# A mixture-of-experts encoder layer on one core: one-time work of the early experts gathered into the first five, and the branch over extra blocks right behind them

## The chip, the cores and the metric

The kernel runs on one core of a Trainium2 chip. The metric is the device time of one execution in microseconds, lower is better. Before the change the median of three runs is 1279.49 us (1279.22 to 1279.97).

## What is computed

One encoder layer over 256 tokens of width 1024, all in float32: a mixer (differential attention beside a two-way state space scan), cross attention over 256 memory tokens, and a mixture of experts, each added to the residual stream; then a final RMSNorm. The change touches the mixture of experts alone:

```python
t = rms_norm(h)                                   # 256 tokens x 1024
top_v, top_i = top_k(t @ w_router + b_router, 4)  # 32 experts
gates = softmax(top_v)
for each expert e and the tokens routed to it:
    hid  = xb @ w_e1[e] + b_e1[e]                 # 1024 -> 2048
    gate = min(hid[:, :1024], 7); lin = clip(hid[:, 1024:], -7, 7)
    act  = gate * sigmoid(1.702 * gate) * (lin + 1)
    y    = act @ w_e2[e] + b_e2[e]                # 1024 -> 1024
h = h + sum over experts of gate_weight * y
out = rms_norm(h, norm_final_g)
```

Each expert has 8 MB in `w_e1` and 4 MB in `w_e2`, and every expert's weights are read once, some 400 MB in all.

## The kernel before

Everything ahead of the experts (mixer, cross attention, router) is straight-line code for the five engines, ordered by semaphores. Then come 32 blocks, one for each expert, of up to 64 tokens. An expert that more than 64 tokens chose would get further blocks, the extra blocks, up to 15 over all experts. How many there are (`n_extra`) is only known on the chip; with the inputs used here there are none, and 32 blocks run.

**Weights.** The weights of an expert are six chunks of 2 MB: four of `w_e1` (numbers 0 to 3) and two of `w_e2` (4 and 5). SyncE issues them in order (`load_block`, `load_chunk`, L308) into a ring of 10 slots, with an eleventh place (`spare`) that serves twice at the start. A slot's next load waits for TensorE to be done with the chunk ten (early on eleven) places earlier (`freed_by`; semaphores `m_w1u` and `m_w2u`). SyncE's program is not touched by the change.

**A block on TensorE** (`block_of`, L1175): four times `hidden_chunk` (16 product instructions of 128x512, L1147), with the hidden bias behind chunk 0 (L1138); then `gather` of the tokens of the next block (L1057), transposes of the gate weights (L574), `scatter` of the previous block's output into the accumulators (L1073), transposes of the hidden values, transposes of the next tokens; then twice `output_part` with a `w_e2` chunk (16 product instructions each, L1169). ScalarE and VectorE do the activation, the selection matrices and the copies between.

**One-time work of the early blocks** is slipped between the chunks of certain blocks by `behind_chunk(early, j)`: two products that add the residual of token tile 1 to its accumulator (`add_residual`, L1023; blocks 3 and 4), the tables of the extra blocks and the transposed gate weights (`extra_block_tables`, block `TABLES_AT` = 5), four products that add the output bias (`add_bias`, L1079; blocks 6 and 7, behind chunks 0 and 2), and the spreading of the final norm's gain (`spread_gain`, L1086; block `GAIN_AT` = 8, behind its first `w_e2` chunk). Behind the latter ScalarE copies the gain out (L1307), and TensorE waits for that copy at the block's end.

**Loops and the branch.** A loop body holds `ROUND` = 5 blocks, since 30 chunks are three turns of the ring. On TensorE blocks 0 to 9 are written out, blocks 10 to 19 are a loop of two rounds, then `n_extra` is loaded into a register (L1274) and a branch follows (L1275). Each of its two arms holds `last_blocks()`: a loop of two rounds (blocks 20 to 29) and the blocks 30 and 31 in an order of their own. The first arm goes on with the code of the extra blocks; the second one is taken here. VectorE writes out blocks 0 to `TABLES_AT` - 1 and ScalarE blocks 0 to `GAIN_AT`, then each has a loop of one block.

Of the kernel before, what the change touches and what calls it, by code (L numbers as in the profile page):

```python
# [42 lines left out]
CHUNKS = W1_CHUNKS + W2_CHUNKS  # L43
ROUND = 5
ROUNDS = NE // ROUND
BRANCH_AT = 4
TABLES_AT, GAIN_AT = 5, 8


C_ID = 0  # L50
# [33 lines left out]
def build(nc, T, out):  # L84

    ctx = ExitStack()
    with ctx:
        def sb(name, cols, parts=P, dt=F32):
            return ctx.enter_context(nc.sbuf_tensor(name, [parts, cols], dt))
# [56 lines left out]
        early = sb("early", 512)  # L146
# [138 lines left out]
        def chunk_at(q, r, j):  # L285

            opening = isinstance(q, int) and q == 0
            n, use = place_at(opening, r, j)
            return n, 16 * use if opening else (q * (CHUNKS * ROUND // RING) + use) * 16
# [9 lines left out]
        def last_chunk_at(b, j):  # L299

            n = LAST.index((b, j)) - len(SPARE_USES)
            return n % RING, (ROUNDS * (CHUNKS * ROUND // RING) + n // RING + 1) * 16
# [259 lines left out]
        def _(pe):  # L562
# [458 lines left out]
            def add_residual(t, n, start):  # L1021

                pe.matmul(pt[(PA, PB)[t]][:, 512 * n:512 * (n + 1)], ident, h3[:, t, 512 * n:512 * (n + 1)],  # L1023
                          start=start, stop=False)
# [52 lines left out]
            def add_bias(t, n):  # L1077

                pe.matmul(pt[(PA, PB)[t]][:, 512 * n:512 * (n + 1)], gT[:, P * t:P * (t + 1)],  # L1079
                          be2[:, 512 * n:512 * (n + 1)], start=False, stop=False)  # L1080

            def spread_gain():
# [4 lines left out]
                                     start=True, stop=True)  # L1087
                last.then_inc(S["ctp"], 1)

            def behind_chunk(early, j):  # L1090

                if early == 3 and j == 3:
                    add_residual(1, 0, False)
                elif early == 4 and j == 1:
                    add_residual(1, 1, False)
                elif early == TABLES_AT:
                    extra_block_tables(j)
                elif early in (6, 7) and j in (0, 2):
                    add_bias(early - 6, j // 2)

            readers[PD] = []
            pe.wait_ge(m_sel, 1)
# [13 lines left out]
            def extra_block_tables(j):  # L1116

                if j == 0:
                    pe.wait_ge(S["ctv"], 1)
                    pe.matmul(pt[PD][0:NE, 0:1], con[0:NE, C_TRI:C_TRI + NE], nbx[:, 0:1], start=True, stop=True).then_inc(S["ctp"], 1)  # L1120
                elif j == 1:
                    pe.wait_ge(S["ctv"], 2)
                    pe.matmul(pt[PD][:, 64:64 + 2 * EXTRA + 1], ones[0:NE, :], blk[:, :], start=True, stop=True).then_inc(S["ctp"], 1)
                elif j == 2:
                    pe.wait_ge(S["ovi"], 1)
                    pe.wait_ge(S["gdv"], NT)
                    for t in range(NT):
                        last = turn(pt[PD][0:NE, 128 + P * t:128 + P * (t + 1)], gate[:, t, :])
                    last.then_inc(S["ctp"], 1)
                else:  # L1130
                    pe.wait_ge(S["gda"], 1)

            def add_hidden_bias():

                for b in range(2):
                    for g in range(2):
                        i = NE * (2 * b + g)
                        pe.matmul(pt[PC][SLOTS * g:SLOTS * (g + 1), 512 * b:512 * (b + 1)], ecol[i:i + NE, :],  # L1138
                                  be1[i:i + NE, :], start=False, stop=False)

            def hidden_chunk(n, j):

                for k in (2 * j, 2 * j + 1):
                    for b in range(2):
                        for g in range(2):
                            c = 2048 * (k % 2) + D * b + 512 * g
                            last = pe.matmul(pt[PC][SLOTS * g:SLOTS * (g + 1), 512 * b:512 * (b + 1)], xT[:, k % 4, k // 4],  # L1147
                                             ring_slot[n][:, c:c + 512], start=(k == 0), stop=(k == KD - 1))
                last.then_inc(m_w1u, 1)
# [25 lines left out]
            def block_of(it, q, r, early=None):  # L1175

                pe.wait_ge(m_xT, 1 if early == 0 else it + 2)
                for j in range(W1_CHUNKS):
                    n, loaded = chunk_at(q, r, j)
                    pe.wait_ge(s_chunk[n], loaded)  # L1180
                    if early == 0 and j == 1:
                        pe.wait_ge(m_xT, 2)
                    if j == 1:
                        add_hidden_bias()
                    hidden_chunk(n, j)
                    behind_chunk(early, j)

                pe.wait_ge(m_sel, it + 2)
                gather()

                if early != 0:
                    pe.wait_ge(m_y, it)
                turn_weights(it)

                if early != 0:
                    pe.wait_ge(m_gs, it)
                    scatter(False, start=(1,) if early == 1 else ()).then_inc(m_sc, 1)

                turn_hidden(it)
                pe.wait_ge(m_xn, it + 2)  # L1200
                turn_block(xgn_early if early == 0 else xgn)

                pe.wait_ge(m_hT, it + 1)
                pe.wait_ge(m_gs, it + 1)
                for g in range(W2_CHUNKS):
                    n, loaded = chunk_at(q, r, W1_CHUNKS + g)
                    pe.wait_ge(s_chunk[n], loaded)
                    output_part(n, g, hT, 512, range(4))
                    if early == GAIN_AT and g == 0:
                        spread_gain()  # L1210
                if early == GAIN_AT:
                    pe.wait_ge(S["acopy"], 7)

            def last_blocks():

                with pe.Fori(BRANCH_AT, ROUNDS) as q:
                    for r in range(ROUND):
                        block_of(q * ROUND + r, q, r)
                a, b = NE - 2, NE - 1
                pe.wait_ge(m_xT, a + 2)  # L1220
                for j in range(W1_CHUNKS):
                    n, loaded = last_chunk_at(0, j)
                    pe.wait_ge(s_chunk[n], loaded)
                    if j == 1:
                        add_hidden_bias()
                    hidden_chunk(n, j)
                pe.wait_ge(m_sel, a + 2)
                gather()
                pe.wait_ge(m_y, a)
                turn_weights(a)  # L1230
                pe.wait_ge(m_gs, a)
                scatter(False).then_inc(m_sc, 1)
                turn_hidden(a)
                pe.wait_ge(m_xn, a + 2)
                turn_block()

                pe.wait_ge(m_hT, a + 1)
                pe.wait_ge(m_xT, b + 2)
                for j in range(W1_CHUNKS):
                    n, loaded = last_chunk_at(1, j)  # L1240
                    pe.wait_ge(s_chunk[n], loaded)
                    if j == 1:
                        add_hidden_bias()
                    hidden_chunk(n, j)
                pe.wait_ge(m_gs, a + 1)
                turn_weights(b)

                for g in range(W2_CHUNKS):
                    n, loaded = last_chunk_at(0, W1_CHUNKS + g)
                    pe.wait_ge(s_chunk[n], loaded)  # L1250
                    output_part(n, g, hT_wait, 0, range(4))
                    if g == 0:
                        turn_hidden(b)

                pe.wait_ge(m_hT, b + 1)
                pe.wait_ge(m_gs, b + 1)
                for g in range(W2_CHUNKS):
                    n, loaded = last_chunk_at(1, W1_CHUNKS + g)
                    pe.wait_ge(s_half[g], 16)
                    output_part(n, g, hT, 512, (0, 1))  # L1260
                    if g == 0:
                        pe.wait_ge(m_y, a + 1)
                        scatter(False, gsc=gsc_wait).then_inc(m_sc, 1)
                    pe.wait_ge(s_chunk[n], loaded)
                    output_part(n, g, hT, 512, (2, 3))

            for q in range(2):
                for r in range(ROUND):
                    block_of(q * ROUND + r, q, r, early=q * ROUND + r)
            with pe.Fori(2, BRANCH_AT) as q:  # L1270
                for r in range(ROUND):
                    block_of(q * ROUND + r, q, r)
            pe.wait_ge(S["ovi"], 1)
            n_extra = pe.value_load(idx[0:1, NE + EXTRA + 1:NE + EXTRA + 2], min_val=0, max_val=EXTRA)  # L1274
            with pe.If(n_extra > 0):  # L1275
# [948 lines left out]
```

## Time and profile before

| | us |
|---|---|
| median of three runs | 1279.49 |
| the profiled execution, whole | 1279.54 |
| its span (first to last instruction) | 1277.6 |
| around the span | 1.9 |
| TensorE busy in the span | 1241.8 |
| VectorE, ScalarE, GpSimd busy | 410.7, 170.8, 113.3 |

The span is cut into 40 slices of 31.9 us on the page. The experts begin at 365 us, in slice 11 (counted from 0), and last to the end. The chain that ended last is made of TensorE for 83% and of DMA for 12%. TensorE's busy time includes the time in which one matmul fills while another drains, so that a busy TensorE isn't one at its peak. The mean granted clock of TensorE is 0.997.

### The profile page before, as it was taken

How to read it: one execution, taken by the hardware profiler on the slowest of the kernel's cores; microseconds unless marked ns; L12 is line 12 of the kernel's file. 1: busy time of each engine (PE TensorE's matmuls, PEld its weight loads, DVE VectorE, ACT ScalarE, POOL GpSimd, SP SyncE). 2: the span in 40 equal slices, each digit the busy share in tenths (PEclk: the TensorE clock that was granted, in tenths of full speed). 3: DMA queues.
4: the chain of work that ended last, by engine and by line, in shares of the span. 5: the costliest groups of instructions: out<-in, count | busy, mean ns of one | idle time of the engine just before them, and what ended most of it. 6: DMA issues, size and time to landing. Idle time of an engine off the chain costs nothing.

```text
span 1277.6 us, 15129 instructions
## 1 busy us (share of the span) xinstructions
PE 1241.8 (97%) x6111; PEld 559.7 (44%) x6111; DVE 410.7 (32%) x845; ACT 170.8 (13%) x299; POOL 113.3 (9%) x107
## 2 busy tenths in 40 slices
PE   8999999999999999999999999999999999999997
PEld 4478886759543333333333333333333333333332
DVE  6789685367432111111121111121111112111111
ACT  2043333011221000000100000000000000000002
POOL 4599400020000000000000000000000000000000
PEclk9999999999999999999999999999999999999999
DMA  8743476692789999999999999999999999999996
GB/s 247 183 165 132 99 137 243 216 311 86 305 349 429 426 427 428 429 426 428 428 428 427 426 428 428 428 428 429 427 426 427 428 427 429 428 428 429 428 427 255
DMA packets 55603, 455.96 MB, mean 357 GB/s; under 512 B 4840, under 2 KB 7088, under 8 KB 30720
## 3 DMA queue, kind: packets, MB, share of 16 engines
q1 hardware_dynamic: 52736, 450.80, 86.0%
q0 software_dynamic: 1664, 3.90, 2.3%
q10 hardware_dynamic: 1152, 0.52, 0.3%
q8 instruction: 40, 0.66, 0.2%
q14 instruction: 11, 0.09, 0.0%
HBM read 453.07 MB, written 1.61 MB: 356 GB/s over the span
## 4 chain that ended last, share of the span: by engine, by line
PE 83%; DMA 12%; DVE 2%; ACT 2%; issue 1%; SPq 0%; DVEq 0%
PE pt L1147 29%; PE pt L1169 16%; PE pt L609 9%; PE pt L596 4%; PE pt L1073 4%; PE pt L574 4%; PE pt L636 4%; PE pt L1057 4%; DMA ring<-in_w_e 3%; DMA stage<-in_w_e 3%; DMA low<-in_w_e 3%; PE pt L1138 2%; PE pt L646 2%; DMA stage<-in_w_xq 2%; ACT wi_ L1307 1%
## 5 line engine op out<-in xcount | busy, mean ns | idle before, releaser
L1147 PE MATMUL pt<-ring,uT_ 128*64 128x512 f32 x1264 | 282.3, 595 | 6.7 <-DMA ring<-in_w_e 5.9
L1147 PEld LDWEIGHTS pt<-ring,uT_ 128*64 128x64 f32 x1264 | 88.2, 137 | 192.7 <-issue 177.8
L2068 DVE COPY ct_<-ct_ 128x2 f32 x31 | 5.2, 169 | 451.6 <-PE pt L1147 444.2
L1169 PE MATMUL pt<-ring,wi_ 128*64 128x512 f32 x560 | 124.5, 596 | 3.7 <-ACT wi_ L1307 3.7
L1147 PE MATMUL pt<-stage,uT_ 128*64 128x512 f32 x400 | 91.3, 603 | 5.2 <-issue 3.7
L1147 PE MATMUL pt<-low,uT_ 128*64 128x512 f32 x384 | 86.3, 595 | 1.5 <-DMA low<-in_w_e 1.5
L609 PE MATMUL pt<-spare,stage 128*128 128x256 f32 x384 | 84.2, 380 | 0.0
L1490 ACT ACTIVATE wi_<-pt 128x512 f32<-128x512 f32 x32 | 19.1, 597 | 472.1 <-PE pt L1147 472.1
L2150 DVE TENSOR_SCALAR wi_<-pt 128x512 f32<-128x512 f32 x32 | 22.1, 692 | 184.9 <-PE pt L1147 184.9
L609 PEld LDWEIGHTS pt<-spare,stage 128*128 128x128 f32 x384 | 72.6, 190 | 10.5 <-issue 0.7
L1169 PEld LDWEIGHTS pt<-ring,wi_ 128*64 128x64 f32 x560 | 39.0, 137 | 77.0 <-issue 72.0
L1073 PE MATMUL pt<-early,lamb 64*128 64x512 f32 x248 | 61.6, 615 | 0.7 <-ACT early L1307 0.7
L596 PE MATMUL pt<-stage,spare 128*128 128x512 f32 x128 | 57.0, 608 | 2.0 <-DMA stage<-in_w_in 2.0
L1057 PE MATMUL pt<-hres,ct_ 128*64 128x512 f32 x248 | 58.5, 593 | 0.0
L1147 PEld LDWEIGHTS pt<-stage,uT_ 128*64 128x64 f32 x400 | 28.3, 139 | 65.8 <-issue 62.6
L1147 PEld LDWEIGHTS pt<-low,uT_ 128*64 128x64 f32 x384 | 26.7, 137 | 58.8 <-issue 55.5
L1307 ACT ACTIVATE early<-pt 128x512 f32<-128x512 f32 (+1 forms) x33 | 19.5, 591 | 224.5 <-PE pt L1169 220.8
L1169 PE MATMUL pt<-stage,wi_ 128*64 128x512 f32 x208 | 46.3, 596 | 1.3 <-ACT wi_ L1307 1.3
L2095 DVE TENSOR_TENSOR uT_<-pt,gains 128x512 f32<-128x512 f32 (+1 forms) x33 | 22.3, 675 | 71.6 <-PE pt L574 71.6
L1169 PE MATMUL pt<-low,wi_ 128*64 128x512 f32 x192 | 42.5, 596 | 1.3 <-ACT wi_ L1307 1.3
L596 PEld LDWEIGHTS pt<-stage,spare 128*128 128x128 f32 x128 | 24.8, 195 | 32.9 <-issue 30.7
L1138 PE MATMUL pt<-uT_,ct_ 32*64 32x512 f32 x256 | 34.8, 613 | 0.2
(347 smaller groups left out, 1237.5 us busy)
## 6 DMA issues: line engine op xcount, KB each, us to landing
ring<-in_w_e SPq DMA_DIRECT2D x114, 2048.0 KB, 26.2
low<-in_w_e SPq DMA_DIRECT2D x38, 2048.0 KB, 25.8
stage<-in_w_e SPq DMA_DIRECT2D x36, 2048.0 KB, 27.7
stage<-in_w_in SPq DMA_DIRECT2D x16, 1024.0 KB, 7.3
stage<-in_w_xkv SPq DMA_DIRECT2D x8, 1024.0 KB, 5.2
ring<-in_w_mix_out SPq DMA_DIRECT2D x4, 1024.0 KB, 9.3
stage<-in_w_xq SPq DMA_DIRECT2D x4, 1024.0 KB, 18.3
ring<-in_w_xo SPq DMA_DIRECT2D x4, 1024.0 KB, 7.3
```

Of the source, the lines that this page charges most:

```text
L574: return pe.transpose(dst, src, ident[0:n, 0:n])
L596: last = pe.matmul(pt[u][:, 512 * t:512 * t + 512], xT[:, k, t * P:(t + 1) * P], w[:, k % 4, :], start=(k == 0), stop=(k == 4 * len(ws) - 1))
L609: last = pe.matmul(pt[u][:, L * m:L * m + L], w[:, k % 4, m * P:(m + 1) * P], xT[:, k, :], start=(k == 0), stop=(k == 4 * len(ws) - 1))
L636: last = pe.matmul(dst, x[:, k, :], w[:, k, :], start=(k == 0), stop=(k == 3))
L646: last = pe.matmul(dst[:, P * m:P * (m + 1)], w[:, k, P * m:P * (m + 1)], x[:, k, :], start=(k == 0), stop=(k == 3))
L1057: last = pe.matmul(pt[PD][SLOTS * n:SLOTS * (n + 1), 0:512], sel[:, t, :], h3[:, t, 512 * n:512 * (n + 1)], start=(t == 0), stop=(t == NT ...
L1073: last = pe.matmul(pt[(PA, PB)[t]][:, 512 * n:512 * (n + 1)], gsc[SLOTS * n:SLOTS * (n + 1), t], ysb[SLOTS * n:SLOTS * (n + 1), :], start= ...
L1138: pe.matmul(pt[PC][SLOTS * g:SLOTS * (g + 1), 512 * b:512 * (b + 1)], ecol[i:i + NE, :], be1[i:i + NE, :], start=False, stop=False)
L1147: last = pe.matmul(pt[PC][SLOTS * g:SLOTS * (g + 1), 512 * b:512 * (b + 1)], xT[:, k % 4, k // 4], ring_slot[n][:, c:c + 512], start=(k == ...
L1169: last = pe.matmul(pt[PD][SLOTS * h:SLOTS * (h + 1), at:at + 512], hidden[:, c, g], ring_slot[n][:, D * c + 512 * h:D * c + 512 * (h + 1)] ...
L1307: return act.activation(dst, src, ACT.Copy)
L2095: return dve.tensor_tensor(xT[:, lo:hi], src, g3[:, lo:hi].to_broadcast([P, hi - lo, 2, SLOTS]), ALU.mult)
```

## The change

The tables move from block 5 to block 1, the gain from block 8 to block 4, the residual products from blocks 3 and 4 to block 2, the bias products from blocks 6 and 7 to blocks 2, 3 and 4. Only blocks 0 to 4 are written out on TensorE, the loop of two rounds (blocks 10 to 19) is gone, the branch stands behind block 4, and the loop in each arm has five rounds (blocks 5 to 29). By the same constants VectorE writes out block 0 alone, and ScalarE blocks 0 to 4.

```diff
-BRANCH_AT = 4
-TABLES_AT, GAIN_AT = 5, 8
+TABLES_AT, GAIN_AT = 1, 4
...
+            BIAS_AT = {(2, 3): (0, 0), (3, 1): (0, 1), (3, 3): (1, 0), (4, 1): (1, 1)}
+
             def behind_chunk(early, j):
 
-                if early == 3 and j == 3:
-                    add_residual(1, 0, False)
-                elif early == 4 and j == 1:
-                    add_residual(1, 1, False)
-                elif early == TABLES_AT:
+                if early == TABLES_AT:
                     extra_block_tables(j)
-                elif early in (6, 7) and j in (0, 2):
-                    add_bias(early - 6, j // 2)
+                elif early == 2 and j < 2:
+                    add_residual(1, j, False)
+                elif (early, j) in BIAS_AT:
+                    add_bias(*BIAS_AT[early, j])
...
             def last_blocks():
 
-                with pe.Fori(BRANCH_AT, ROUNDS) as q:
+                with pe.Fori(1, ROUNDS) as q:
                     for r in range(ROUND):
                         block_of(q * ROUND + r, q, r)
...
-            for q in range(2):
-                for r in range(ROUND):
-                    block_of(q * ROUND + r, q, r, early=q * ROUND + r)
-            with pe.Fori(2, BRANCH_AT) as q:
-                for r in range(ROUND):
-                    block_of(q * ROUND + r, q, r)
+            for r in range(ROUND):
+                block_of(r, 0, r, early=r)
             pe.wait_ge(S["ovi"], 1)
```

## Rows read from the trace of the kernel before

**Rows 1.** The page: span, and GB/s of the DMA engines in 40 slices.
```profile
span 1277.6 us, 15129 instructions
...
GB/s 247 183 165 132 99 137 243 216 311 86 305 349 429 426 427 428 429 426 428 428 428 427 426 428 428 428 428 429 427 426 427 428 427 429 428 428 429 428 427 255
```
**Rows 2.** Chain that ended last, blocks 1 and 2 (start us, us, what).
```profile
421.19 3.43 PE pt L1147 x16
...
448.54 3.43 PE pt L1147 x16
```
**Rows 3.** The same chain, its late part.
```profile
1066.54 42.42 DMA low<-in_w_e
...
1125.29 42.43 DMA stage<-in_w_e
```
**Rows 4.** The same chain: the one-time work, and block 5's first and block 6's first chunk.
```profile
463.44 1.06 PE pt L1023 x2
...
505.67 3.44 PE pt L1147 x16
...
534.13 3.43 PE pt L1147 x16
537.56 1.05 PE pt L1079 x2
...
617.27 1.91 PE pt L1086 x4
619.18 3.58 PE pt L1169 x16
```
**Rows 5.** SyncE's loads (L308), issue and landing: 340:360, then single chunks.
```profile
L308 SPq DMA_DIRECT2D ring<-in_w_e x3: 328/328/328, 346.3 to 358.0; - x3
...
DMA to landing us min/median/max: 7.6/8.9/8.9
...
L308 SPq DMA_DIRECT2D ring<-in_w_e x1: 333/333/333, 473.9 to 473.9; - x1
...
DMA to landing us min/median/max: 10.4/10.4/10.4
...
L308 SPq DMA_DIRECT2D stage<-in_w_e x1: 332/332/332, 509.3 to 509.3; - x1
...
DMA to landing us min/median/max: 14.1/14.1/14.1
...
L308 SPq DMA_DIRECT2D ring<-in_w_e x1: 332/332/332, 530.9 to 530.9; - x1
...
DMA to landing us min/median/max: 12.1/12.1/12.1
```
**Rows 6.** Timeline of ScalarE, 610:625 (bracket: idle before, releaser).
```profile
619.21 1.02 ACT L1307 ACTIVATE spare<-pt 128x1024 f32<-128x1024 f32 x1 [5.65 <-PE pt L1086]
```
**Rows 7.** The branch: L1274 and L1275, TensorE's timeline, and windows (clock before DMA share).
```profile
L1274 PEldq TENSOR_LOAD <-idx x1: 490/490/490, 919.6 to 919.6; - x1
...
L1275 PEldq COMPARE_BRANCH  x1: 6449/6449/6449, 920.5 to 920.5; - x1
...
927.52 5.22 PE L1147 MATMUL pt<-stage,uT_ 128*64 128x512 f32 x16 [3.68 <-issue]
...
928.00:932.00 4.00, 4.00 (x14) 1.14 (x12) 0.00 (x0) 0.00 (x0) 0.00 (x0) 0.66 1.01 422
```
**Rows 8.** DMA queues in 484:779, then in 790:920 (packets, MB, share).
```profile
q8 instruction: 11, 0.18, 0.2%
...
q1 hardware_dynamic: 3824, 55.69, 100.7%
```
**Rows 9.** Landing of the chunks issued at 756.4 and at 893.2 us.
```profile
DMA to landing us min/median/max: 23.1/23.1/23.1
...
DMA to landing us min/median/max: 33.1/33.1/33.1
```

## The prediction

> **What bounds the kernel now.** I read the page's rate row first [rows 1]: from slice 12 on (383 us) the DMA engines move 426 to 429 GB/s in every slice, up to the last one. Slices 10 and 11 have 305 and 349. So from shortly after the experts begin, the stream of weight chunks has no gap, and at 428 GB/s a chunk of 2.097 MB takes 4.90 us, the six of a block 29.4 us. The chain of waits gives the other side. In blocks 1 and 2 it is TensorE end to end, and from one block's first chunk to the next one's there are 448.54 - 421.19 = 27.35 us [rows 2]. TensorE is thus 2.0 us a block faster than the stream. It starts with eleven chunks in hand and eats that lead up. From 1066 us on the chain holds two DMA pieces of 42.4 us, 1125.29 - 1066.54 = 58.75 us apart, which is twelve chunks of 4.90 us [rows 3]: there TensorE waits for the stream.
>
> The end of the kernel is therefore the end of the stream plus a fixed tail. TensorE's time in the early blocks is of no account by itself. It matters by one route only: a chunk is issued when TensorE frees a slot, and if TensorE frees so late that the DMA engines run dry, the stream loses that time for good.
>
> How near to dry they are can be read from issue and landing. A chunk that meets idle queues lands 7.6 to 8.9 us after its issue (three of them at 346 to 358 us, where the rate row is below its plateau) [rows 1, 5]. What a chunk takes beyond that is the work still queued ahead of it, its slack. The early blocks have little, with 7.6 as the price of an empty queue [rows 5]:
>
> - issued at 473.9 (freed by block 3's first output chunk, after 9 to 10 us in which nothing is freed): 10.4 - 7.6 = 2.8 us
> - issued at 509.3 (freed by block 5's chunk 0): 14.1 - 7.6 = 6.5 us
> - issued at 530.9 (freed by block 5's first output chunk): 12.1 - 7.6 = 4.5 us
>
> **The change part by part.** The loss of the stream is the largest value, over all issues, of (how much later TensorE frees the slot than before) minus (slack of that issue). So I need the lateness.
>
> Moved work. One residual product costs 1.06 us, one bias product 1.05 us, the gain 1.91 us; the tables are the difference between block 5 and a plain block, (534.13 - 505.67) - 27.35 = 1.11 us [rows 2, 4]. The whole is 1.1 + 2 x 1.06 + 4 x 1.05 + 1.9 = 9.3 us, before as after, but before only 2.1 of it (the residual) lay ahead of block 5. After, all does. Lateness at the end of block 2: 1.1 + 2.1 + 1.05 = 4.3 us. At block 3's first output chunk two more bias products are in and one residual product is no longer there: 4.3 + 2.1 - 1.06 = 5.3 us. At the end of block 4: 9.3 - 2.1 = 7.2 us. Waits that these pieces add are covered: the table steps of VectorE and the copy of the transposed gates each lie under a chunk of 3.4 us, as they do now in block 5, whose surplus of 1.11 us holds any that is not. SyncE's program stays, so nothing is moved past its queue. That VectorE's and ScalarE's loops begin earlier I count at nothing: both engines wait for TensorE for most of each block, from 0 to at most the 0.1 us that a turn of TensorE's own loop shows.
>
> The branch. Now TensorE's sequencer enters it at 920.5 us and comes out 6.45 us later [rows 7]. The array still had work until 3.68 us before 927.52, that is to 923.84, so the sequencer led by 3.34 us and the gap is the rest, 6.45 - 3.34 + 0.57 to the first product = 3.68 us. The granted clock then shows 0.66 in 928 to 932 us, a mix of the full 2.4 and of 1.2 GHz after that idle time, and the first 16 products take 5.22 instead of 3.43 us: 1.79 us more [rows 2, 7]. Together 5.5 us, at a place where the slack has grown to more than 25 us (a chunk issued at 893.2 takes 33.1 us) [rows 9], so it is free today. In block 5 it is not.
>
> There it is also dearer. The branch follows block 4, which now ends in the wait for the gain's copy. That copy ends 1.02 + 0.03 us after the gain's products, and 3.58 us of output products follow these [rows 4, 6]. The register load begins then and the branch 0.9 us later (919.6 to 920.5) [rows 7]. So the lead is 3.58 - 1.05 - 1.0 = 1.5 us instead of 3.3, the gap 6.45 + 0.57 - 1.5 = 5.5, and with the slow clock the branch costs 7.3 us. Bounds: nothing, if the target's code should be at hand; 6.45 + 0.57 + 1.8 = 8.8 us with no lead at all. I take 7.3, since the row that comes nearest is a branch of the same form over the same kind of code.
>
> The Trainium skill (Runtime: NRT & Kernel Launch, section Instruction fetch mechanics) says that a taken branch to a page that is not held forces a DMA fetch before the engine can go on, and prefers unrolled code for that; the 6.45 us agree. It speaks against moving the branch under the thin queue.
>
> Loss. Block 3: 5.3 - 2.8 = 2.5 us. Block 5, chunk 0: 7.2 + 7.3 - 6.5 = 8.0 us. Block 5, first output chunk, where the tables of block 5 have dropped out: 14.5 - 1.1 - 4.5 = 8.9 us. In block 6 the lateness falls by the 2.1 us of bias that was there, in block 7 again, and the slack stays, so 8.9 is the largest.
>
> A gain of the stream. Ten blocks' worth of instructions is no longer fetched: blocks 5 to 14 now pass through new code and then blocks 20 to 24 do again behind the branch; after, only blocks 5 to 9 do. Eleven packets of instructions come between 484 and 779 us, none in 790 to 920, the loop's second round [rows 8]. With them 60 chunks land in 779.5 - 484.3 = 295.2 us, 4.920 each (issues 473.9 and 756.4); without them 30 chunks in 926.3 - 779.5 = 146.8 us, 4.893 each (issues 756.4 and 893.2) [rows 5, 9]. That is 1.6 us for eleven, 0.15 each, and 1.5 us for the ten that go.
>
> The same page's section also has it that TensorE's instruction memory is refilled in sequence and a loop profits from no cache. By this the ten fetches would be made anyway and the sum would be 1.5 us higher. The row of 790 to 920 us, with no instruction packet over four and three quarters blocks, speaks against it here.
>
> Sum: 1279.54 + 8.9 - 1.5 = **1286.9 us**. The profiled execution is 0.05 us above the median of the runs, so both serve as the base. TensorE's own lateness at the end of block 19 is down to the 1.8 us by which the branch got dearer, and it then meets the later stream a few blocks earlier than now.
>
> **The rivals.** *Cover holds* (not slower). The chunks that TensorE has in hand hide everything: the queue never runs dry, and the change only saves fetches. 1279.54 - 1.5 = 1278.0 us. For it: the stream's plateau is unbroken over 850 us [rows 1] and TensorE has time to spare by the end. Against it: that reserve lies in the ring, not in the queue. It decides at the issue now at 473.9: if this chunk still meets more than 2.5 us of queue behind the moved work, the case is on its way to hold.
>
> *Cheap branch.* The moved work drains the queue in block 3, but the branch costs nothing, since its target is at hand or the fetch is quick while the queue is thin: 1279.54 + 2.5 - 1.5 = 1280.5; with half its price 1283. For it: the fetch was seen once only, with 30 us of loads queued. Against: the 6.45 us of that one.
>
> *Dear branch.* No lead of the sequencer (8.8 us) and an empty queue at the price of 8.9 instead of 7.6 us: 7.2 + 8.8 - 1.1 - (12.1 - 8.9) = 11.7, so 1279.54 + 11.7 - 1.5 = 1289.7; without the fetch saving 1291.2. For it: two of the three early chunks took 8.9 [rows 5].
>
> **How the numbers follow.** Forecast 0.70, cover holds 0.10, cheap branch 0.10, dear branch 0.10. A measurement of this kernel tells 0.2%, 2.6 us, from no change. Cover holds and most of the cheap branch lie within that: same 0.16. Faster needs the cover and more than the fetches: 0.02. Slower 0.82. The range goes from 1281.5, inside the cheap branch, to 1290.5, inside the dear one.
>
> **What would show it.** Right: the issue of block 3's first output chunk some 5 us later than 473.9 and landing in about 7.6 to 8 us; the stream's rate in slices 14 to 16 below 426; two drops, the larger one in the gap of 5.5 us behind block 4, with a branch of about 6.4 us there; the late chain with the same 42.4 us pieces, about 7 us later; 10 or so fewer packets on the instruction queue. Wrong: no landing below 9 us between 440 and 600 us, a rate row without a dent, or an end that is set by TensorE and not by the stream.

## The result: 0.8% slower, from stalls of the weight stream in two stretches

| | us |
|---|---|
| before, median of six runs | 1279.36 |
| after, median of six runs | 1289.64 (1287.76 to 1291.39) |
| ratio | 1.008, 95% interval 1.0065 to 1.0096 |
| predicted | 1286.9, range 1281.5 to 1290.5 |
| profiled execution after | 1289.69, span 1287.8 |

The page after. The rate row has three dents that [rows 1] hasn't: slices 14, 16 and 17, with 367, 328 and 420 GB/s. Slice 15 between them and the plateau behind them are the old ones, so the stream lost time in two stretches (block 2's end to block 3, and block 4's end to block 5) and won little of it back.

```profile
span 1287.8 us, 15190 instructions
...
GB/s 245 182 164 132 101 154 227 240 307 82 305 367 429 428 367 428 328 420 428 426 428 428 429 427 430 427 428 429 427 430 427 428 430 426 430 428 428 427 427 260
```

The late chain of waits (start us, us, what) is the one of [rows 3], the same 42.4 us pieces, 10.2 us later:

```profile
1076.76 42.46 DMA low<-in_w_e
...
1135.55 42.45 DMA stage<-in_w_e
```

SyncE's loads after (L307 is the old L308), with the time from issue to landing. The one that was issued at 473.9 and the one at 509.3 in [rows 5] now meet an empty queue, 7.8 and 7.6 us; the one of 530.9 takes 9.8.

```profile
L307 SPq DMA_DIRECT2D ring<-in_w_e x1: 333/333/333, 478.8 to 478.8; - x1
...
DMA to landing us min/median/max: 7.8/7.8/7.8
...
L307 SPq DMA_DIRECT2D stage<-in_w_e x1: 333/333/333, 524.5 to 524.5; - x1
...
DMA to landing us min/median/max: 7.6/7.6/7.6
...
L307 SPq DMA_DIRECT2D ring<-in_w_e x1: 333/333/333, 545.0 to 545.0; - x1
...
DMA to landing us min/median/max: 9.8/9.8/9.8
```

The branch, and the chain around it:

```profile
L1270 PEldq COMPARE_BRANCH  x1: 6492/6492/6492, 511.0 to 511.0; - x1
```
```profile
507.14 1.91 PE pt L1085 x4
509.05 3.58 PE pt L1168 x16
512.64 5.40 issue
518.04 6.30 PE pt L1146 x16
```

It lasts as long as before (6.49 against 6.45 us), 1.6 us of it under the last products. The idle gap is 5.40 us against 3.68 in [rows 7], and the 16 products behind it take 6.30 us against 5.22.

**One scale for all kernels.** The part ahead of the experts differs by some us between executions of the same code. I therefore count from the issue of the first load that an expert's product frees, 371.63 us before and 370.78 after:

```profile
371.63 0.33 SPq L308 DMA_DIRECT2D ring<-in_w_e  x1
```
```profile
370.78 0.33 SPq L307 DMA_DIRECT2D ring<-in_w_e  x1
```

"Late" is how much later than before a load is issued on this scale, "lost" how much later it lands. The three places are the loads of [rows 5] (block 3's first output chunk, block 5's chunk 0, block 5's first output chunk). Landings are read to 0.1 us, so "lost" is good to about that. "End" is the end of the span on the same scale. For example, late at the first place: (478.76 - 370.78) - (473.85 - 371.63) = 5.8 us.

| kernel | late, lost 1 | late, lost 2 | late, lost 3 | end | median ratio to before (95%) |
|---|---|---|---|---|---|
| after | 5.8, 3.3 | 16.1, 9.6 | 15.0, 12.6 | +11.1 | 1.008 (1.0065 to 1.0096) |
| work moved alone | 5.8, 3.1 | 7.8, 4.8 | 6.7, 4.8 | +4.8 | 1.0035 (1.002 to 1.0049) |
| after without branch | 5.8, 3.1 | 7.8, 5.1 | 6.7, 5.1 | +3.6 | 1.001 (0.9997 to 1.0023) |
| gain in block 3 | 5.8, 4.4 | 9.0, 5.8 | 7.9, 5.8 | +3.2 | 1.0024 (1.0011 to 1.0038) |
| the same, again | 5.8, 3.3 | 8.9, 5.3 | 7.8, 5.3 | +3.6 | 1.0042 (1.0025 to 1.0059) |
| branch behind block 9 | 0, -0.3 | 0, -0.3 | 0, -0.3 | -0.5 | 0.9998 (0.9983 to 1.0012) |
| 5 idle products, block 3 | 4.3, 2.2 | 4.3, 2.5 | 4.3, 2.9 | +3.8 | 1.0016 (1.0001 to 1.0032) |
| 10 idle products, block 3 | 8.6, 6.0 | 8.6, 6.9 | 8.6, 8.0 | +7.9 | 1.005 (1.0035 to 1.0064) |
| 5 idle products, block 9 | 0, 0.7 | 0, 0.7 | 0, 0.7 | +0.6 | 0.9987 (0.9972 to 1.0002) |
| wait in the arm | 5.8, 3.2 | 14.3, 8.0 | 13.2, 10.9 | +9.7 | 1.0061 (1.0034 to 1.0087) |
| later entry | 5.8, 3.3 | 15.4, 8.9 | 14.3, 11.6 | +10.2 | 1.0088 (1.0058 to 1.0118) |
| after, again | 5.8, 3.3 | 15.9, 9.4 | 14.8, 12.2 | +10.7 | 1.0091 (1.0063 to 1.0119) |

Two limits of this table. One profiled execution can be off by a microsecond: eight of its kernels are 5.8 us late at the first place, and seven of them lose 3.1 to 3.3 us there, but the gain in block 3 lost 4.4 in its first profile (that load took 9.0 us to land, the others 7.7 to 8.0). And the medians are coarse too: the runs of the kernel before lie in two groups, around 1277.5 and 1281.5 us.

### The profile page after: what moved, and what is told of

Same layout as the page of the kernel before. It is cut to its first block, busy times and chain, and to the rows that moved or that the text cites. A ratio compares the mean times of both kernels' runs of the same rounds, so it can differ in the third digit from the quotient of the medians.

```text
span 1287.8 us, 15190 instructions
## 1 busy us (share of the span) xinstructions
PE 1244.1 (97%) x6111; PEld 558.6 (43%) x6111; DVE 411.0 (32%) x845; ACT 170.8 (13%) x299; POOL 113.3 (9%) x107
## 4 chain that ended last, share of the span: by engine, by line
PE 79%; DMA 17%; ACT 2%; issue 1%; DVE 1%; SPq 0%; DVEq 0%; ACTq 0%
PE pt L1146 25%; PE pt L1168 15%; DMA ring<-in_w_e 10%; PE pt L608 10%; PE pt L635 6%; PE pt L595 4%; PE pt L1072 4%; PE pt L573 4%; PE pt L1056 3%; DMA low<-in_w_e 3%; DMA stage<-in_w_e 3%; PE pt L645 2%; PE pt L1137 2%; ACT wi_ L1302 1%; DMA stage<-in_w_in 1%
```

## The experiments

### Work moved, branch left

```diff
-TABLES_AT, GAIN_AT = 5, 8
+TABLES_AT, GAIN_AT = 1, 4
 (and behind_chunk of the change; BRANCH_AT stays 4)
```

> The kernel before, with the one-time work moved as in the change (tables in block 1, residual in 2, bias in 2 to 4, gain in 4), the branch left behind block 19. Queue theory (the loss is the largest lateness of a freed slot minus the slack of its load): 5.3 - 2.8 = 2.5 us lost at block 3's first output chunk and no more, so 2 to 3 us above before, and that chunk lands about 2.4 us later than before, after 7.6 to 8 us. Rival 'branch alone' (moved work costs nothing): 0. Rival 'work alone' (the moved work makes the whole loss): about 10 us.

Measured: +4.8 us on the scale, ratio 1.0035 (+4.5 us). "Branch alone" and "work alone" are both out. The queue is empty at block 3, as expected, with 3.1 us lost there. The 2.5 us that I had expected were too few by 0.6 at this place, and I had expected nothing at the next one: 1.7 us more go at the two loads that block 4's output products free, and these don't meet an empty queue:

```profile
L308 SPq DMA_DIRECT2D low<-in_w_e x1: 332/332/332, 506.6 to 506.6; - x1
...
DMA to landing us min/median/max: 9.3/9.3/9.3
```

By the price of 7.6 us this load had 1.7 us of slack, and yet it landed 0.9 us behind the pitch of 4.9 from its predecessor; so did the next one, with 9.6 us. An instruction packet is fetched in this stretch (500 to 516 us):

```profile
q8 instruction: 1, 0.02, 0.4%
```

### The change without the branch

```diff
-            with pe.If(n_extra > 0):
-                last_blocks()
-                ...
-            with pe.If(n_extra < 1):
-                last_blocks()
+            last_blocks()
...
```

The load of `n_extra` into a register goes too.

> The changed kernel without TensorE's branch: it leaves out the arm for extra blocks (there are none) and goes from block 4 straight into the loop of five rounds. Queue theory: 2.5 us lost in block 3, nothing at block 5 (lateness 7.2 - slack 6.5 = 0.7 is less than 2.5), and 1.5 us or a little more given back by instruction packets that are not fetched: 0 to 1.5 us above before, 9 us below the changed kernel. Rival 'work alone': still 10 us above before. Rival 'branch alone': 1.5 us below before.

Measured: lost at the three places as with the work moved alone (3.1, 5.1, 5.1), end +3.6 us. So the branch in its new place makes 12.6 - 5.1 = 7.5 us of the loss. The loss of 5.1 us is twice the 2.5 that I had expected, for the same reasons as in the run before. The fetches that fall away give back 5.1 - 3.6 = 1.5 us. In the medians it lies 8.8 us below after and 1.5 us above before (3.6 on the scale); its interval against before takes in no change. Its profiled execution is a high one among its runs (1286.11 us), in part because what lies ahead of the experts was 3 us longer, which is why the scale is needed.

### The gain in block 3

```diff
-TABLES_AT, GAIN_AT = 1, 4
+TABLES_AT, GAIN_AT = 1, 3
```

> The changed kernel with the norm's gain spread in block 3, not 4, so that block 4 no longer ends in the wait for its copy and the sequencer can enter the branch about 3.3 us ahead of the array, not 1.6. If the lead counts: idle gap behind block 4 3.7 us instead of 5.4, half clock for 3.4 us instead of 6.8 and so 1.8 us of slow products instead of 2.9: 2.8 us less than the changed kernel, 7.4 above before. Rival (the wait for the copy has no part in it, the instruction fetch sets the gap): gap 5.4 us and time as in the changed kernel.

Measured: 7.6 us below after, not 2.8 (5.4 when both kernels were run again, 7.1 to 7.9 on the scale). I had only thought of the sequencer's lead. It did rise, to 3.56 us, but the branch itself also got shorter, 4.00 us instead of 6.49:

```profile
L1270 PEldq COMPARE_BRANCH  x1: 3999/3999/3999, 512.5 to 512.5; - x1
```
```profile
516.11 0.94 issue
517.05 3.65 PE pt L1146 x16
```

The gap is 0.94 us and no product behind it is slow. So the branch's duration is no constant of the branch.

### The branch behind block 9

```diff
-BRANCH_AT = 4
+BRANCH_AT = 2
...
-            with pe.Fori(2, BRANCH_AT) as q:
-                for r in range(ROUND):
-                    block_of(q * ROUND + r, q, r)
```

> The kernel before with the one-time work where it was, the branch behind block 9 and one loop of four rounds in each arm (the loop of blocks 10 to 19 gone). Queue theory: at block 10 a load has 10 us of slack and the branch makes TensorE 5.5 us late, so nothing is lost; five instruction packets fewer give 0.75 us: 1278.6, within 1 us of before. Rival 'an early branch costs its time anywhere': 5.5 us above before.

Measured: TensorE is 5.3 us late behind the branch, and nothing is lost (0.1 us at block 10's loads); end -0.5 us, ratio 0.9998. Here, where the queue was some 10 us deep, the early branch was free. This kernel has the smaller code and the old time; it does not beat the kernel before by anything that can be measured.

### Idle products: five and ten in block 3, five in block 9

```diff
+            def idle_products(n):
+                for _ in range(n):
+                    pe.matmul(pt[PD][:, 0:512], ident, h3[:, 1, 0:512], start=True, stop=True)
...
                 if early == 3 and j == 3:
                     add_residual(1, 0, False)
+                    idle_products(5)    # 10; or 5 at (early, j) = (9, 3)
```

> The kernel before with five idle products (128x512, into tiles of PSUM that nobody reads then) behind chunk 3 of block 3: 5.3 us more work for TensorE, at one place. Queue theory: the load issued in before at 473.9 has 2.8 us of slack, so 2.5 us are lost there, and up to 1 us more at the next block's first output chunk (5.3 us late against 3.6 + 2.5 us of slack, nearly empty, which the moved work alone showed to cost 0.9): 2.5 to 3.5 us above before. Rival 'TensorE's work counts wherever it is': 5.3 us.

> The same with ten idle products, 10.6 us. Queue theory: 10.6 - 2.8 = 7.8 us lost, with the nearly empty queue behind it up to 9: the second five products cost their whole 5.3 us, where the first five cost half. Rival: 10.6 us, the two fives cost the same.

> Five idle products as in the first of these, but in block 9. Queue theory: the loads there have 7 us of slack and more, so nothing is lost: 0, within 1 us. Rival 'TensorE's work counts wherever it is': 5.3 us.

In a row such products cost less than one alone, 4.46 us for five:

```profile
460.88 1.12 PE L1023 MATMUL pt<-hres,con 128*128 128x512 f32 x2
461.84 4.46 PE L1093 MATMUL pt<-hres,con 128*128 128x512 f32 x10
```

So the lateness is 4.3 and 8.6 us, and less the slack of 2.8 us the first place should lose 1.5 and 5.8. It shows 2.2 and 6.0, and against what already stood at the end of block 2 (1.0 and -0.3 us, ahead of the idle products) 1.2 and 6.3. At this place the second five thus cost all that they are late, the first five a quarter to a half. By the end the kernels are 3.8 and 7.9 us later, so the first five have cost 2.8 to 3.8 of 4.3 us. The medians give +0.8, +5.3 and, with block 9, -2.4 us against the kernel before: 4.5 us for the second five, and too coarse for the first five alone. In block 9 they made TensorE 4.6 us late at block 10's loads and lost nothing: 0.7 us stood before them, 0.6 at the end. The rival that counts TensorE's work wherever it is falls.

### The wait for the gain's copy behind the branch

```diff
-                if early == GAIN_AT:
-                    pe.wait_ge(S["acopy"], 7)
...
             def last_blocks():
 
+                pe.wait_ge(S["acopy"], 7)
                 with pe.Fori(1, ROUNDS) as q:
```

> The changed kernel with the wait for the gain's copy taken from the end of block 4 to the first place in either arm of the branch: all work, and its order, stay. If the lead of the sequencer over the array sets the gap: the branch begins at least 3.3 us ahead of the array's end, lasts 6.4 us again, the gap falls from 5.4 to 3.6 us, and the slow products cost at most 1.8 instead of 2.9 us: 2 to 3 us less than the changed kernel, about 1287. If the branch's fetch waits for what the DMA queues hold at that moment and the earlier entry finds them as thin as the kernel with the gain in block 3 did: branch of 4 us, no gap to speak of, 7 us less, about 1282. Rival (the lead plays no part): as the changed kernel, 1289.6.

Measured: 1287.23 us, 2.4 below after (1.4 on the scale). The lead rose to 2.7 us (not 3.3), the branch took 7.02 us, the gap was 4.80 and the products behind it took 5.07 us:

```profile
511.63 4.80 issue
516.43 5.07 PE pt L1146 x16
```

The lead counts, by about its own length, and does not explain the gain in block 3.

### The gain in block 3, with a later entry into the branch

```diff
                 block_of(r, 0, r, early=r)
+            pe.wait_ge(m_w2u, W2_CHUNKS * (ROUND - 1) + 1)
             pe.wait_ge(S["ovi"], 1)
```

> The kernel with the gain in block 3, and TensorE's sequencer held ahead of the branch until the products with block 4's first w_e2 chunk are done (a wait on TensorE's own count). All work stays. The branch is then entered 2.6 us ahead of the array's end and about 1 us behind the issue of the load that those products free, where the kernel with the gain in block 3 entered it 0.3 us ahead of that issue. If the fetch of the branch's target waits for loads already queued on the DMA engines: the branch takes 6.4 us again and not 4.0, the gap is about 4.4 us, with slow products behind it, and the time 4 to 5 us above that of the kernel with the gain in block 3, about 1286.5. Rival (only the lead counts, the fetch is as quick as there): branch 4.0 us, gap 1.9 us, time 1 us above, about 1283.

> The kernel with the gain in block 3 once more, on the same chip as the one with the later entry: if the quick branch belongs to its place in the order of the loads, it takes 4.0 us again (rival: it was chance, and the branch takes 6.4 us in this profile).

> The changed kernel once more, as a base on the same chip: branch of 6.5 us, gap of 5.4 us, 10 us above before. If the half clock behind the gap has no fixed length, it may show 3.4 instead of 6.8 us of it here.

Measured: the same work, entered 0.7 us behind the issue of the load that block 4's first output products free (508.30 and 509.04 us) instead of 0.3 us ahead of it (512.86 and 512.55 us). The branch takes 6.67 us, the gap is 4.66 and the slow products are back:

```profile
L1271 PEldq COMPARE_BRANCH  x1: 6674/6674/6674, 509.0 to 509.0; - x1
```
```profile
511.55 4.66 issue
516.21 6.35 PE pt L1146 x16
```

Run beside it on the same chip, the kernel with the gain in block 3 took 3.88 us for the branch again, and after took 6.12. The medians are 1290.2 for the later entry (3.7 us more than I expected, over five runs that reach from 1285.7 to 1294.0), 1284.7 and 1290.1. On the scale the later entry loses 6.6 us more than its pair (+10.2 against +3.6), where the lead alone (2.5 us against 3.6) can make 1.1. So the entry relative to the load decides here. What it changes is the work that is queued: at the entry the load issued last was 2.8 and 3.2 us from its landing in the two quick cases, but 6.2 us in after, 8.0 in the later entry and 8.4 with the wait in the arm. The order alone is not enough: behind block 9 the branch was also entered 0.3 us ahead of the next load (649.08 and 649.39 us), with 10.1 us queued, and it was slow:

```profile
L1272 PEldq COMPARE_BRANCH  x1: 6431/6431/6431, 649.1 to 649.1; - x1
```

The traces also tell when the code came. In after the queue view has no instruction packet between 511 and 515.1 us and one in 515.1 to 516.2; in the quick branch of the gain in block 3 it lies in 514.05 to 515.2:

```profile
q8 instruction: 1, 0.02, 5.7%
```
```profile
q8 instruction: 1, 0.02, 5.9%
```

It begins 4.1 us behind the entry (511.05 us) in after, 4.3 in the later entry, 4.7 with the wait in the arm and 4.0 in the kernel before, and 1.6 and 1.4 us behind it in the two quick cases. In all of them, and behind block 9, the branch is over 1.4 to 1.5 us after the end of that packet. So the branch waits for its code, and the difference lies ahead of the packet. But the packet does not wait for all that is queued: in the kernel before 31.5 us were queued, and it came after 4.0. What sets this upper end, these runs don't show.

## Why the prediction was right, and where its sizes were off

The time lies inside the range, but near its upper end: 7.4 us more than before were forecast, and 10.3 were measured (10.15 in the profiled executions).

**Right.** What bounds the kernel, the route of the loss and its form. The stream is lost at the places named: the queue ran empty at the loads of block 2's end, block 3 and block 5, and the late chain came with the same pieces. The lateness of TensorE at block 3 was 5.8 us (5.3 foretold), the branch 6.49 us (6.45), the lead 1.6 (1.5), the gap 5.40 (5.5). The saving on instruction fetches was 1.4 us: 12.5 us are lost at block 12's loads, 11.1 at the end, where the kernel before has made its fetches behind the branch. I had 1.5 for it, and packets on the instruction queue from 378 to 1100 us are 11 instead of 22:

```profile
q8 instruction: 11, 0.18, 0.1%
```

"Cover holds" fell, since no reserve in the ring helped. The time itself is that of "dear branch", 1289.7. It had the same route with dearer terms, and two of them came nearer than mine: the branch with its slow products cost 16.1 - 7.8 = 8.3 us (it had 8.8, I had 7.3), and the slack at the place of the largest loss was 2.4 us (it had 3.2, I had 4.5). Its condition, a sequencer with no lead, did not hold, since the lead was 1.6 us; that it meets the number to 0.1 us is luck. "Cheap branch" fell for this kernel, but its reason turned out true of a neighbour: with a thin queue and the entry ahead of the next load the fetch is quick.

**Mis-sized.** The sum had a loss of 8.9 us at block 5's first output chunk; the row shows 12.6. Two terms make the 3.7 us.

- *The slack of 4.5 us* was really 15.0 - 12.6 = 2.4. I took 7.6 us, the least landing, as the price of an empty queue, and kept 8.9 for the range only. A load that is issued while the one ahead of it is about to land took more: the one of block 4's first output products took 8.1 to 11.0 us in the ten profiles in which TensorE was late there (9.9 in after), and landed 5.1 to 7.3 us behind its predecessor instead of 4.9, although it seemed to have slack. That is 2.1 us here, and 1.7 of the 2.3 us that the moved work alone cost above the 2.5. An instruction packet lies near such places, but no run separated its part.
- *The lateness of 13.4 us* was 15.0. Of the 1.6 us, 1.0 is the branch: 1.1 us more for the products behind the gap, 6.30 instead of 5.22 us (I had carried over the slow stretch of a gap of 3.68 us to one of 5.4), less 0.1 us of gap. The other 0.6 is the moved work, 7.8 us at the end of block 4 and not 7.2. I had priced each inserted product by its own row, but what follows it takes 0.15 us more: a chunk 3.58 instead of 3.43 us, the gather 1.87 instead of 1.72. In block 2, before and after:

```profile
425.64 10.45 PE pt L1147 x48
436.09 1.72 PE pt L1057 x8
```
```profile
426.94 3.58 PE pt L1146 x16
430.53 1.05 PE pt L1022 x2
431.58 7.02 PE pt L1146 x32
438.60 1.05 PE pt L1078 x2
439.65 1.87 PE pt L1056 x8
```

The residual product that stands beside the hidden bias adds 1.06 us of lateness, the next one and the bias product 1.21 each, and in block 4 the gain 2.06 instead of 1.91. Four such places (the second residual product, the first two bias products, the gain) make the 0.6 us.

The end would have been 1279.54 + 12.6 - 1.5 = 1290.6 by these terms; the part ahead of the experts happened to be 0.85 us shorter in the profiled execution, which gives its 1289.7. The Trainium skill (Runtime: NRT & Kernel Launch, Instruction fetch mechanics) says: "Prefetch is purely sequential — there's no instruction cache that benefits from spatial locality." Read as saying that a loop is fetched anew in every round, it is not borne out: after the first of five rounds, which ends near 655 us, no instruction packet comes until 1100 us. Its other rule, that a taken branch to code that is not held waits for a fetch, is: the branch was over 1.4 us behind the landing of an instruction packet.

One label to set right: the two lines of [rows 2] are the first chunks of blocks 2 and 3. The 27.35 us between them are a block without one-time work all the same.

## What to carry to other kernels

Where a prefetched stream sets the end, don't ask what a piece of work costs its engine. Ask how deep the DMA queue is at the loads that the engine issues late. That depth is the time from issue to landing less what an empty queue takes; it was 2.8 us in block 3, where of 8.6 us of delay 6 were lost, while in block 9 a delay of 4.6 us was free. Keep one-time work, waits at block ends and taken branches out of the stretch in which this number is below their sum, and allow some 2 us more, as here, for a queue that is nearly empty. Price a piece of inserted work by how much later the next load is issued, not by its own row alone.

## What was not expected of the hardware

- The same branch behind block 4 took 6.1 to 7.0 us when entered behind the issue of a load, 3.9 and 4.0 us when entered just ahead of it with 3 us of loads queued. With 10 to 36 us queued the branch of the other kernels took 5.9 to 6.5 us.
- The products behind the branch's idle gap of TensorE, 16 of them: 3.65 us (full clock) behind gaps of 0.88, 0.94 and, once, 3.48 us; 5.07 to 5.35 us behind gaps of 3.09, 3.37, 3.68 and 4.80 us; 6.30 to 6.53 us behind 3.53, 4.66, 5.01 and 5.40 us. The granted clock falls from 2.4 to 1.2 GHz in the latter two groups. The gap's length does not fix it: 4.80 cost less than 4.66, and 3.48 cost nothing where 3.53 cost the most. What does, these runs don't show.

The chain around the gap in the kernel with the work moved alone, 3.48 us and no slow product, and in the one with five idle products in block 3:

```profile
922.37 3.48 issue
925.86 3.65 PE pt L1147 x16
```
```profile
925.63 3.53 issue
929.16 6.53 PE pt L1155 x16
```
